# Modulation products moved to other stages of a two-block network

## The chip, the cores and the metric

One core of a Trainium2 chip runs the whole program in one launch. The metric is the device time of the kernel in microseconds, lower is better; the median of three runs is given. A trace comes from one profiled execution.

## The reference

Two blocks of a network run one after the other on x, 256 tokens by 2048, all in float32. The first has two layers: differential attention and, after a shared K and V product, forgetting attention. The second is a state-space (S5) mixer with a gate and an MLP with squared relu. What is moved here is the *modulation*: a vector c goes through silu and is multiplied with a large matrix, and slices of the result shift, scale and gate the tokens.

```
c_act = jax.nn.silu(c)
for l in range(DEPTH):                                  # 2 layers
    mod = c_act @ w_mod[l] + b_mod[l]                   # [2048] @ [2048, 6144]
    shift, scale, gate = jnp.split(mod, 3, axis=-1)
    h = x * (1.0 + scale[:, None]) + shift[:, None]
    if l < N_A:
        y = diff_attention(h, a_w_in[l], a_w_out[l], ...)
    else:
        k_sh, v_sh, F_sh = shared_kv(x, c_act, kv_w_mod, kv_b_mod, kv_w, kv_b_f)
        y = forgetting_attention(h, b_w_in[l - N_A], b_w_out[l - N_A], k_sh, v_sh, F_sh)
    x = layer_norm(DN_ALPHA * x + gate[:, None] * y, ln_g[l], ln_b[l])
...
sh1, sc1, gt1, sh2, sc2, gt2 = adaln(c, w_mod[layer], b_mod[layer])    # [2048] @ [2048, 12288], second block
```

## The kernel before

**Modulation.** All modulation matrices together are cut into 56 pieces of 2048 x 512 weights, 4 MiB each, listed in MODS in the order in which they are used: m0s (0 to 7), m2a (8 to 15), m0g (16 to 19), m1s (20 to 27), kv (28 to 35), m1g (36 to 39), m2b (40 to 51), m2c (52 to 55). One piece is one call of mod(j), which exists in four programs. SP loads it as four quarters of 1 MiB. TensorE (line 2064) first calls sums(j - 1), which reduces the row that ScalarE copied for the piece before into the bank MB0, and then multiplies the four quarters with the padded vector cpad, 32 records in the trace, each quarter as it lands. ScalarE (line 974) copies the bank into mod_rows. When a group is complete, VectorE adds its bias (mod_bias, line 1412), after a wait for the group's last sums.

**The ring.** All weights of the kernel pass through a ring of six slots of 1 MiB. The table made by tables() gives every load its slot in one fixed order; SP issues the loads in that order, and before each it waits until TensorE has used up the slot's last contents (place, line 597). So at most six quarters are ahead of TensorE, and a load that stands early in the order holds up those behind it.

**The stages around the change**, in order of time:
- Projections and state matrices, until about 738 us in the trace.
- The first attention block (lines 2308 to 2340): a software pipeline of 21 stages t over 16 tiles. In stage t TensorE multiplies a tile's weights with v (ao, tile t - 5), turns them (at, tile t - 4) and makes the scores (as, tile t); VectorE and ScalarE make the softmax between. It begins with loads of the projections that the kernel itself stored earlier (proj_d, 2 MiB each): 0 and 1 before it (lines 639, 640), 2 and 3 (lines 645, 650) after waits of SP on semaphores of small stores by GpSimd and on TensorE. VectorE starts when the last store of m_state has landed. The result is normed per head and turned (to_T, transposes on TensorE).
- Steps 0 to 3 (the product with a_w_out), then the first layer norm on VectorE, and steps 4 to 19 (q, g, k, v). A step is multiply(n): 4 MiB of weights in four quarters, split by ScalarE and VectorE into a high and a low part (w_hi, w_lo), and 96 matmuls of 128x512. Inside step 0 VectorE waits for x, which GpSimd loads once oT has been turned. After the layer norm GpSimd stores x (2 MiB, line 825), and TensorE turns it for step 4 (turn_in).
- The second attention block, steps 20 to 23, the second layer norm.
- The v stage (lines 2413 to 2418): 16 loads of 1 MiB of m_state through the ring, 8 chunks for each half f; ScalarE copies each chunk's result out (v_out). Then, for each f, a scan of 32 states on VectorE, each copied by ScalarE (states_out, line 1196).
- The y stage on TensorE (from line 2421), and the steps of the gated product and the MLP.

**Where mod(j) is called** is given by the dictionaries of lines 67 to 73: after a projection panel, after a chunk of the state matrices, in stage t of the first attention (MOD_AT_A), after step n (MOD_AT_STEP), at the layer norms (MOD_AT_LN), after each half of the v stage (MOD_AT_V) and in the second attention (MOD_AT_B). SP, ScalarE and TensorE follow the same dictionaries in their programs.

Of the kernel before, what the change touches and what calls it, by code (L numbers as in the profile page):

```python
# [60 lines left out]
MOD_END = {g: max(j for j, (h, _) in enumerate(MODS) if h == g) for g, _ in MODS}  # L61
# [4 lines left out]

MOD_AT_PRE = {**{pn: 8 + pn for pn in range(8)}, 9: 16, 11: 17}
MOD_AT_BL = {0: 18, 9: 19, 10: 20, 19: 21, 20: 22}
MOD_AT_A = {5: 23, 9: 24, 13: 25}
MOD_AT_STEP = {0: 26, 1: 27, 2: 28, **{n: 26 + n for n in range(4, 17)}, 55: 52, 56: 53, 57: 54, 58: 55}  # L70
MOD_AT_LN = ((29,), (48, 49))
MOD_AT_V = (50, 51)
MOD_AT_B = {2 + 6 * i: 43 + i for i in range(5)}
SUMMED = ("m0s", "m2b", "m2c")


# [12 lines left out]
N_Q, N_K, N_W1, N_GLU, N_MLP, NS = 4, 12, 20, len(FRONT), len(FRONT) + len(GLU), len(STEPS)  # L89
# [19 lines left out]
def tables():  # L109
# [8 lines left out]
    def mod(j):  # L118
        load("mod", j)
        bank.use(("mod", j), GM)  # L120
# [97 lines left out]
    for f in range(2):  # L218
        for i in range(8):
            ring.use(("ms", f, i), slots)  # L220
            bank.use(("vl", f, i), GV)
        mod(MOD_AT_V[f])
    for f in range(2):
        for i in range(8):
            ring.use(("cl", f, i), slots, 2)
# [18 lines left out]
def build(nc, A, out):  # L244
    ctx = ExitStack()
    with ctx:
# [77 lines left out]
        def reg(off, n):  # L324
            return AR[:, off:off + n]
# [267 lines left out]
        def sync_program(sp):  # L593
# [20 lines left out]
            def mod(j):  # L614
                load_w(("mod", j), MOD_W[MODS[j][0]], 0, 128 * MODS[j][1])
# [22 lines left out]
            sp.wait_ge(*filled("proj", 15, 1))  # L638
            sp.dma_start(reg(24576, 4096), proj_d[0]).then_inc(S["p0"], 16)
            sp.dma_start(reg(12288, 4096), proj_d[1]).then_inc(S["p1"], 16)  # L640
            sp.wait_ge(S["st0"], 16 * 8)
            sp.wait_ge(S["st1"], 16 * 8)
            sp.wait_ge(S["st2"], 16 * 8)
# [4 lines left out]
            sp.wait_ge(S["st2"], 16 * 10)  # L648
            sp.wait_ge(S["blm"], 32)
            sp.dma_start(reg(4096, 4096), proj_d[3]).then_inc(S["p3"], 16)  # L650
            for t in sorted(MOD_AT_A):
                mod(MOD_AT_A[t])

            W_OF = {"wout0": (A["a_w_out"][0], 0), "q": (A["b_w_in"][0], 0), "g": (A["b_w_in"][0], 2048), "k": (A["kv_w"], 0),
# [33 lines left out]
            for f in range(2):  # L688
                for i in range(8):
                    dst, sem = place("ms", f, i)  # L690
                    d0 = 64 * (i // 4) + 32 * f + 8 * (i % 4)
                    sp.dma_start(dst, m_state_d[:, d0 * 256:d0 * 256 + 2048]).then_inc(sem, 16)
                mod(MOD_AT_V[f])
            sp.wait_ge(S["cl0"], 16 * 16)
            sp.wait_ge(S["cl1"], 16 * 16)
            sp.wait_ge(S["toep"], 16 * 64)
# [146 lines left out]
        def scalar_program(a):  # L843
# [130 lines left out]
            def mod(j):  # L974
                a.wait_ge(*filled("mod", j))
                if j:
                    a.wait_ge(S["mod_sum"], j)
                copy(ROWS[:, :], bank("mod", j)[:, :], *empty("mod", j))
# [132 lines left out]
            for t in range(21):  # L1111
                if 0 <= t - 5 < 16:
                    i = t - 5
# [7 lines left out]
                if 0 <= t - 1 < 16:  # L1121
                    i = t - 1
# [31 lines left out]
            for t in range(35):  # L1154
                if 0 <= t - 2 < 32:
                    i = t - 2
# [5 lines left out]
                if 0 <= t - 1 < 32:  # L1162
                    i = t - 1
# [50 lines left out]

            for i in range(8):
                v_step(0, i)
            mod(MOD_AT_V[0])
            states_out(0, lambda i: v_step(1, i), 3)
            mod(MOD_AT_V[1])
            states_out(1, lambda i: y_step(0, i), 4)  # L1220
            for i in range(0, 8, 2):
                y_step(1, i)
# [60 lines left out]
        def vector_program(v):  # L1283
# [501 lines left out]
            for t in range(21):  # L1785
                if 0 <= t - 3 < 16:

                    i = t - 3
# [8 lines left out]
                if 0 <= t - 4 < 16:  # L1797
                    i = t - 4
# [5 lines left out]
                if 0 <= t - 1 < 16:  # L1804
                    i = t - 1
# [49 lines left out]
            v.wait_ge(S["x1"], 16)  # L1855
            v.wait_ge(*emptied("bc", "m0g", 3))
            for n in range(N_W1):
                if n == N_Q - 1:
                    mod_bias("m1s")
                if n == N_Q:  # L1860
                    layer_norm(0)
                    own()
                    ts(sc1, M("m1", 16), 1.0, None, ADD, None, *o.up("scol"))
                    split_in("q", h_raw["q"], sc1, M("m1", 0), AHk, ALk, N_Q, 8 * n)
                    scan_ctx(2)
                elif n == N_K:
                    v.wait_ge(*emptied("xt", "q", 7))
                    v.wait_ge(*filled("step", N_K - 1, 1))
                    own()
                    ts(sc1, M("kv", 16), 1.0, None, ADD, None, *o.up("scol"))  # L1870
                    split_in("k", h_raw["k"], sc1, M("kv", 0), AHk, ALk, N_K)
                    v.wait_ge(*filled("zf"))
                    v.wait_ge(S["zf"], 32)
                    tt(zz, bank("zf")[:, 0:32].rearrange("p (t h) -> p t h", t=2), bf.unsqueeze(1).to_broadcast([128, 2, 16]), ADD,
                       *empty("zf"))
                    own()
                    ts(tz, zz, -1.0, None, MUL, None)
                    own()
                    tt(tz, tz, zz, MIN, *o.up("zt"))
                    ts(lf, zz, 0.0, None, MIN, None)  # L1880
                    v.wait_ge(S["zl"], 1)
                    own()
                    tt(lf, lf, tz, SUB, *o.up("lf"))
                round_of(n, n in (N_Q - 1, N_W1 - 1))
                if n == N_K - 2:
                    mod_bias("kv")
                elif n == N_K + 2:
                    mod_bias("m1g")
            v.wait_ge(*filled("nFT"))
            ts(nFT[0:16, :], bank("nFT")[0:16, 0:256], -1.0, None, MUL, None, *empty("nFT"))  # L1890
# [2 lines left out]
            for t in range(35):  # L1893
                if 0 <= t - 3 < 32:
                    i = t - 3
# [8 lines left out]
                if 0 <= t - 1 < 32:  # L1904
                    i = t - 1
# [129 lines left out]
        def tensor_program(p):  # L2035
# [15 lines left out]
            def sums(j):  # L2051

                group, nt = MODS[j]
                p.wait_ge(*emptied("mod", j))
                ended = sum(1 for g_ in MOD_GROUPS if MOD_END[g_] < j)
                if j == MOD_FIRST[group] and ended:
                    p.wait_ge(S["mod_bias"], ended)
                c_ = mod_c(j)
                for i in range(4):
                    c0 = 256 + 2 * (nt + i) if group == "m2a" else mod_base(j) + i  # L2060
                    t = mm(MB0[:, c0:c0 + c_.stop - c_.start], ROWS[:, 128 * i:128 * i + 128], sel[:, c_], True, True)
                t.then_inc(S["mod_sum"], 1)

            def mod(j):

                if j and j - 1 not in [MOD_END[g_] for g_ in SUMMED]:
                    sums(j - 1)
                for q in range(4):
                    w = chunk("mod", j, q)
                    p.wait_ge(*landed("mod", j, q))  # L2070
                    if q == 0:
                        room("mod", j)
                    for i in range(4):
                        t = mm(bank("mod", j)[32 * i:32 * i + 32, :], cwide[:, 4 * q + i, :], w[:, i, :], q == 0, q == 3)
                    t.then_inc(*(fill("mod", j) if q == 3 else (S["taken"], 1)))
# [109 lines left out]
            for j in range(8):  # L2185
# [4 lines left out]
                if j == 4:  # L2190
                    p.wait_ge(S["lam_cols"], 1)
                    room("lam")
                    for i, s_ in enumerate((cr, ci, lbr, lbi)):
                        t = tr(bank("lam")[:, 128 * i:128 * i + 128], s_)
# [55 lines left out]
            def u_sums(run):  # L2250

                room("ss", run)
                if run == 0:
                    p.wait_ge(S["sq"], 1)
                    p.wait_ge(S["sq_even"], 1)
                    mm(bank("ss", 0)[:, 0:8], sel[:, :], ssu, True, True).then_inc(*fill("ss", 0))
                else:
                    p.wait_ge(S["ss_rows"], 2)
                    for t2 in range(2):
                        t = mm(bank("ss", 1)[:, 0:8], to_chunk[:, t2].rearrange("p a t c -> p (a t c)"), ss_rows[:, t2, :],  # L2260
                               t2 == 0, t2 == 1)
                    t.then_inc(*fill("ss", 1))
# [4 lines left out]
            for b in range(8):  # L2267
                t = mm(bank("fu")[:, 64 * b:64 * b + 64], spread[:, b, :, :].rearrange("p q h -> p (q h)"), u_cols, True, True)
# [21 lines left out]
            for b in range(33):  # L2290
                if b < 32:
                    p.wait_ge(S["blm"], b + 1)
                    for r in range(2):
                        room("bl", b, r)
                        for j in range(4):
                            t = tr(bank("bl", b, r)[:, 128 * j:128 * j + 128], bls[b % 2][r][:, 128 * j:128 * j + 128])
# [13 lines left out]
            for t_ in range(21):  # L2310
                if 0 <= t_ - 5 < 16:
                    i = t_ - 5
# [5 lines left out]
                    for s in range(t2 + 1):  # L2318
                        t = mm(bank("ao", i)[:, 0:256], a_av(i)[:, 128 * s:128 * s + 128], vN[0][:, s, 256 * h:256 * h + 256],
                               s == 0, s == t2)  # L2320
                    t.then_inc(*fill("ao", i))
                if 0 <= t_ - 4 < 16:
                    i = t_ - 4
                    p.wait_ge(S["amix"], i + 1)
                    room("at", i)
                    for s in range(i % 2 + 1):
                        t = tr(bank("at", i)[:, 128 * s:128 * s + 128], wk[i % 4][:, 128 * s:128 * s + 128])
                    t.then_inc(*fill("at", i))
                if t_ < 16:
# [3 lines left out]
                    for c in range(2):  # L2333
                        t = mm(bank("as", t_)[:, 256 * c:256 * c + w_], qT[0][:, 2 * h + c, 128 * t2:128 * t2 + 128],
                               kT[0][:, 2 * h + c, 0:w_], True, True)
# [37 lines left out]
            for t_ in range(35):  # L2373
                if 0 <= t_ - 3 < 32:
                    i = t_ - 3
# [30 lines left out]
                multiply(n)  # L2406
            for j in MOD_AT_LN[1]:
                mod(j)
            u_sums(1)
            for pc in range(8):  # L2410
                u_turn(1, pc)
            p.wait_ge(S["u_made"], 16)
            for f in range(2):
                for i in range(8):
                    p.wait_ge(*landed("ms", f, i))
                    v_chunk(("vl", f, i), slot("ms", f, i).rearrange("p (d r m) -> p d r m", d=8, r=2), UL,
                            64 * (i // 4) + 32 * f + 8 * (i % 4))
                mod(MOD_AT_V[f])
            sums(MOD_END["m2b"])
            p.wait_ge(S["zeroed"], 1)  # L2420
            for f in range(2):
                p.wait_ge(S["copied"], 32 * (f + 1))
# [90 lines left out]
```

## Time and profile before

| | us |
|---|---|
| Median of three runs | 2861.78 (2855.18 to 2862.5) |
| The profiled execution's own time | 2862.5 |
| Its span in the trace | 2860.7 |
| TensorE busy | 2583.2 (90%) |
| VectorE busy | 1578.2 (55%) |
| ScalarE busy | 1098.3 (38%) |
| Moved by DMA | 699.74 MB, 245 GB/s on average |

The shares are averages over stages that differ: what counts for a moved piece of work is what bounds the stage that it leaves and the stage that it enters.

### The profile page before, as it was taken

The page shows a single profiled execution, that of the slowest core. Times are in us where ns is not written, and L with a number is a line of the kernel's source. Part 1 is how long each engine was busy: PE and PEld are TensorE (multiplying, and loading weights), DVE is VectorE, ACT ScalarE, POOL GpSimd, SP SyncE. Part 2 cuts the span into 40 slices and gives each one's busy share as a digit, 9 for nine tenths or more (in the row PEclk, how much of TensorE's full clock was granted, in tenths as well). Part 3 has the DMA queues.
Part 4 walks back from the last instruction along what each step waited for, and adds up shares of the span by engine and source line. Part 5 has one row for each costly group of instructions (what it writes and reads, how often), then busy time and mean ns, then how long its engine had stood idle before and what let it go on. Part 6 is the DMA issues. An engine that isn't in the chain of part 4 may idle for free.

```text
span 2860.7 us, 42569 instructions
## 1 busy us (share of the span) xinstructions
PE 2583.2 (90%) x17983; PEld 2098.0 (73%) x17983; DVE 1578.2 (55%) x2434; ACT 1098.3 (38%) x1812; POOL 196.9 (7%) x299
## 2 busy tenths in 40 slices
PE   5799999888779799899999877889699999999997
PEld 1588877666557687797757666678598898998885
DVE  4566887788557754333335627354555455554444
ACT  0253333344432333334324327344444443443333
POOL 1112333010100001111000010000000000000000
PEclk8799999899889899899978957999899999999998
DMA  9979999675958689689655687745445555556852
GB/s 354 338 240 332 351 329 323 238 283 214 370 191 310 226 296 345 241 309 347 204 200 197 198 274 277 262 147 176 147 133 191 189 180 191 190 182 234 298 192 82
DMA packets 316574, 699.74 MB, mean 245 GB/s; under 512 B 13568, under 2 KB 14048, under 8 KB 311136
## 3 DMA queue, kind: packets, MB, share of 16 engines
q1 hardware_dynamic: 296992, 625.17, 63.1%
q0 software_dynamic: 19120, 69.75, 7.3%
q8 instruction: 142, 2.33, 0.3%
q10 hardware_dynamic: 272, 2.10, 0.2%
q14 instruction: 48, 0.39, 0.0%
HBM read 646.77 MB, written 56.49 MB: 246 GB/s over the span
## 4 chain that ended last, share of the span: by engine, by line
PE 74%; DVE 12%; DMA 8%; ACT 3%; issue 1%; SPq 1%; DVEq 0%; POOL 0%; ACTq 0%
PE bank L2037 72%; DVE arena L1287 4%; DMA ring<-in_a_w_in 3%; DMA ring<-in_w_mod 3%; DVE ring_lo L1287 2%; PE bank L2040 1%; DVE arena L1295 1%; ACT arena L850 1%; DVE sm L1287 1%; PE bank L2246 1%; DMA ring<-in_a_w_out 1%; DMA arena<-arena 0%; SPq L608 0%; DMA proj<-sm 0%; DMA arena<-in_x 0%
## 5 line engine op out<-in xcount | busy, mean ns | idle before, releaser
L1287 DVE TENSOR_TENSOR ring_lo<-ring,w_hi 128x1024 fp32r<-128x1024 f32 (+1 forms) x384 | 430.9, 1134 | 480.9 <-ACT w_hi L900 455.9
L900 ACT CAST w_hi<-ring 128x1024 fp32r<-128x1024 f32 x320 | 333.5, 1048 | 492.9 <-PE bank L2037 437.5
L1287 DVE TENSOR_TENSOR ring_lo<-ring,att_w_hi 128x1024 fp32r<-128x1024 f32 x192 | 231.0, 1222 | 299.1 <-ACT att_w_hi L900 289.7
L900 ACT CAST att_w_hi<-ring 128x1024 fp32r<-128x1024 f32 x192 | 197.5, 1048 | 380.7 <-PE bank L2037 125.7
L2037 PE MATMUL bank<-in_hi,w_hi 128*128 128x256 f32 x1024 | 290.9, 284 | 1.2 <-DVE n L1292 1.2
L2037 PE MATMUL bank<-in_lo,w_hi 128*128 128x256 f32 x1024 | 290.6, 284 | 0.0
L2037 PE MATMUL bank<-in_hi,ring_lo 128*128 128x256 f32 x1024 | 290.1, 283 | 0.0
L2037 PE MATMUL bank<-ring,cpad 128*32 128x512 f32 x1792 | 244.4, 682 | 28.4 <-DMA ring<-in_w_mod 24.8
L2037 PE MATMUL bank<-w_hi,hid_lo 128*128 128x512 f32 x640 | 257.7, 403 | 3.5 <-DVE ring_lo L1287 3.5
L2037 PE MATMUL bank<-att_w_hi,att_hi 128*128 128x512 f32 x512 | 206.1, 403 | 12.8 <-DVE ring_lo L1287 12.8
L2037 PE MATMUL bank<-ring_lo,att_hi 128*128 128x512 f32 x512 | 202.7, 396 | 0.0
L2037 PE MATMUL bank<-att_w_hi,att_lo 128*128 128x512 f32 x512 | 202.0, 395 | 0.0
L2037 PE MATMUL bank<-w_hi,hid_hi 128*128 128x512 f32 x512 | 201.6, 394 | 0.0
L2037 PE MATMUL bank<-ring_lo,hid_hi 128*128 128x512 f32 x512 | 200.7, 392 | 0.0
L2037 PEld LDWEIGHTS bank<-in_hi,w_hi 128*128 128x128 f32 x1024 | 195.8, 191 | 4.1 <-issue 2.5
L850 ACT CAST in_lo<-ring 128x512 fp32r<-128x512 f32 x192 | 115.4, 622 | 213.1 <-DMA ring<-in_a_w_in 107.2
L2037 PEld LDWEIGHTS bank<-in_hi,ring_lo 128*128 128x128 f32 x1024 | 195.4, 191 | 0.0
L2037 PEld LDWEIGHTS bank<-in_lo,w_hi 128*128 128x128 f32 x1024 | 194.9, 190 | 0.1
L2037 PEld LDWEIGHTS bank<-ring,cpad 128*32 128x32 f32 x1792 | 53.4, 119 | 164.9 <-issue 97.8
L2037 PE MATMUL bank<-w_hi,in_hi 128*128 128x512 f32 x384 | 153.8, 401 | 16.7 <-DVE in_lo L1287 14.4
L1287 DVE TENSOR_TENSOR ring_lo<-ring,in_lo 128x512 fp32r<-128x512 f32 x192 | 129.4, 702 | 70.2 <-ACT in_lo L850 70.0
L2037 PE MATMUL bank<-hid_lo,in_lo 128*128 128x256 f32 x512 | 149.8, 293 | 14.4 <-DVE ring_lo L1287 14.4
(249 smaller groups left out, 5103.2 us busy)
## 6 DMA issues: line engine op xcount, KB each, us to landing
ring<-in_w_mod SPq DMA_DIRECT2D x192, 1024.0 KB, 11.5
ring<-in_a_w_in SPq DMA_DIRECT2D x64, 1024.0 KB, 10.4
ring<-in_w_mlp_in SPq DMA_DIRECT2D x64, 1024.0 KB, 5.3
ring<-in_w_mlp_out SPq DMA_DIRECT2D x64, 1024.0 KB, 5.1
ring<-in_kv_w_mod SPq DMA_DIRECT2D x32, 1024.0 KB, 10.6
ring<-in_b_w_in SPq DMA_DIRECT2D x32, 1024.0 KB, 7.0
ring<-in_kv_w SPq DMA_DIRECT2D x32, 1024.0 KB, 6.8
ring<-in_s_w_glu SPq DMA_DIRECT2D x32, 1024.0 KB, 5.3
```

The lines of the kernel that those rows point to most:

```text
L850: return a.copy(dst, src).then_inc(*(to or o.up("act")))
L900: a.copy(whi(h), raw_half(h)).then_inc(*o.up("whi"))
L1287: return v.tensor_tensor(dst, x, y, op).then_inc(*(to or o.up("dve")))
L1295: return v.scalar_tensor_tensor(out=dst, in0=x, scalar=s1, in1=y, op0=o1, op1=o2).then_inc(*(to or o.up("dve")))
L2037: return p.matmul(dst, l_, r_, start=start, stop=stop, skip_group_check=True)
L2040: return p.transpose(dst, src, ident[0:k, 0:k])
L2246: t = p.transpose(bank("u", run, pc)[:, 32 * j:32 * j + 32], HT[run][at, e, j, :, :].rearrange("p q h -> p (q h)"), ident[at, at])
```

## The change

Which stages call mod(j) is changed. The attention block has six of them (23 to 28) in place of three (23 to 25), steps 0 to 2 have none in place of one each, the first layer norm has three (29 to 31) in place of one (29), and the v stage none in place of two. All later places keep their count and take an index that is higher by two, until the second layer norm, which has 50 and 51. SP issues the loads of mod 23 before those of projections 2 and 3. The biases of m1s, kv and m1g are added after earlier steps, and the last sums of m2b are made before u_sums(1).

```diff
-MOD_AT_A = {5: 23, 9: 24, 13: 25}
-MOD_AT_STEP = {0: 26, 1: 27, 2: 28, **{n: 26 + n for n in range(4, 17)}, 55: 52, 56: 53, 57: 54, 58: 55}
-MOD_AT_LN = ((29,), (48, 49))
-MOD_AT_V = (50, 51)
-MOD_AT_B = {2 + 6 * i: 43 + i for i in range(5)}
+MOD_AT_A = {1: 23, 4: 24, 6: 25, 9: 26, 11: 27, 14: 28}
+MOD_AT_STEP = {**{n: 28 + n for n in range(4, 17)}, 55: 52, 56: 53, 57: 54, 58: 55}
+MOD_AT_LN = ((29, 30, 31), (50, 51))
+MOD_AT_B = {2 + 6 * i: 45 + i for i in range(5)}
...
             sp.dma_start(reg(24576, 4096), proj_d[0]).then_inc(S["p0"], 16)
             sp.dma_start(reg(12288, 4096), proj_d[1]).then_inc(S["p1"], 16)
+            mod(MOD_AT_A[1])
             sp.wait_ge(S["st0"], 16 * 8)
...
-            for t in sorted(MOD_AT_A):
+            for t in sorted(MOD_AT_A)[1:]:
                 mod(MOD_AT_A[t])
...
-                mod(MOD_AT_V[f])
...
-            mod(MOD_AT_V[0])
             states_out(0, lambda i: v_step(1, i), 3)
-            mod(MOD_AT_V[1])
             states_out(1, lambda i: y_step(0, i), 4)
...
-                if n == N_Q - 1:
+                if n == 1:
                     mod_bias("m1s")
...
-                if n == N_K - 2:
+                if n == N_Q + 4:
                     mod_bias("kv")
-                elif n == N_K + 2:
+                elif n == N_Q + 8:
                     mod_bias("m1g")
...
             for j in MOD_AT_LN[1]:
                 mod(j)
+            sums(MOD_END["m2b"])
             u_sums(1)
...
-                mod(MOD_AT_V[f])
-            sums(MOD_END["m2b"])
```

## Rows read from the trace of the kernel before

**Rows 1.** The page: the span, and the chain that ended last by engine.
```profile
span 2860.7 us, 42569 instructions
...
PE 74%; DVE 12%; DMA 8%; ACT 3%; issue 1%; SPq 1%; DVEq 0%; POOL 0%; ACTq 0%
```

**Rows 2.** Windows: stretch, length, busy us (x instructions) by engine, PE clock, DMA, GB/s.
```profile
core 0: us, PE busy (x) PEld busy (x) DVE busy (x) ACT busy (x) POOL busy (x), PEclk, DMA share, GB/s
...
748.00:789.00 41.00, 37.79 (x226) 23.79 (x226) 27.13 (x91) 23.30 (x86) 0.00 (x0) 0.92 1.05 384
797.00:815.00 18.00, 12.64 (x64) 10.46 (x63) 14.44 (x34) 8.72 (x20) 0.00 (x0) 0.81 0.00 0
849.00:876.00 27.00, 26.68 (x136) 19.40 (x135) 19.86 (x30) 8.24 (x9) 0.00 (x0) 1.00 0.88 313
932.00:947.00 15.00, 4.21 (x39) 1.49 (x38) 13.87 (x20) 0.99 (x3) 0.00 (x0) 0.72 0.95 331
```

**Rows 3.** Timeline of SP's issues: start, length, what.
```profile
718.00 0.35 SPq L639 DMA_DIRECT2D arena<-proj  x1
...
734.48 37.37 SPq L608 DMA_DIRECT2D ring<-in_w_mod  x12
```

**Rows 4.** DMA view: the total of 718 to 748; slices of 748 to 796.
```profile
DMA packets 1506, 11.27 MB, mean 376 GB/s; under 512 B 159, under 2 KB 159, under 8 KB 993
...
GB/s 406 403 386 387 387 387 386 389 384 386 389 387 386 389 384 386 389 387 389 386 389 389 386 386 387 386 389 386 387 382 230 394 396 405 394 387 384 389 386 280
```

**Rows 5.** Timeline of the first attention block: start, length, engine, what, idle before.
```profile
747.66 0.42 DVE L1295 SCALAR_TENSOR_TENSOR LT<-LT,bank 128x256 f32<-128x256 f32 x1 [15.68 <-DMA m_state<-MSB]
...
759.49 1.06 PE L2037 MATMUL bank<-ring,cpad 128*32 128x512 f32 x8 [0.73 <-DMA ring<-in_w_mod]
...
768.54 0.95 PE L2037 MATMUL bank<-sel,mod_rows 128*128 128x1 f32 x8
...
781.04 0.95 PE L2037 MATMUL bank<-sel,mod_rows 128*128 128x1 f32 x8
...
787.11 0.70 PE L2037 MATMUL bank<-arena,MSB 128*128 128x256 f32 x2
...
807.24 2.79 PE L2040 MATMUL bank<-ident,arena 128*128 128x128 f32 x12 [4.47 <-DVE arena L1295]
```

**Rows 6.** Timeline of TensorE: the mods after steps 0 to 3, the turn.
```profile
848.96 0.95 PE L2037 MATMUL bank<-sel,mod_rows 128*128 128x1 f32 x8
849.84 3.64 PE L2037 MATMUL bank<-ring,cpad 128*32 128x512 f32 x32
...
876.43 0.95 PE L2037 MATMUL bank<-sel,mod_rows 128*128 128x1 f32 x8
...
903.75 0.95 PE L2037 MATMUL bank<-sel,mod_rows 128*128 128x1 f32 x8
...
931.63 0.95 PE L2037 MATMUL bank<-sel,mod_rows 128*128 128x1 f32 x8
...
946.94 5.80 PE L2040 MATMUL bank<-ident,arena 128*128 128x128 f32 x28 [10.79 <-DVE arena L1295]
```

**Rows 7.** Timeline of TensorE: the two mods of the second layer norm.
```profile
1626.40 0.95 PE L2037 MATMUL bank<-sel,mod_rows 128*128 128x1 f32 x8
...
1634.89 1.07 PE L2037 MATMUL bank<-ring,cpad 128*32 128x512 f32 x8 [0.36 <-DMA ring<-in_w_mod]
1638.22 1.94 PE L2037 MATMUL bank<-ring,cpad 128*32 128x512 f32 x8 [2.27 <-DMA ring<-in_w_mod]
```

**Rows 8.** DMA queues of 826 to 836, GpSimd's (q0) and SP's (q1).
```profile
q0 software_dynamic: 398, 3.08, 75.9%
q1 hardware_dynamic: 479, 0.95, 25.5%
```

**Rows 9.** Timeline around the v stage: ScalarE's copies, the sums before the y stage.
```profile
1702.32 1.02 ACT L850 COPY arena<-bank 128x256 f32<-128x256 f32 x2 [2.36 <-PE bank L2037]
1710.63 0.58 ACT L850 COPY mod_rows<-bank 128x512 f32<-128x512 f32 x1 [7.28 <-PE bank L2037]
...
1754.56 1.87 PE L2037 MATMUL bank<-sel,mod_rows 128*128 128x1 f32 x8 [13.16 <-ACT mod_rows L850]
```

More of the change, by code:

```diff
@@ L2417, in tensor_program @@
                             64 * (i // 4) + 32 * f + 8 * (i % 4))
-                mod(MOD_AT_V[f])
-            sums(MOD_END["m2b"])
             p.wait_ge(S["zeroed"], 1)
```

## The prediction

> **What bounds the kernel now.** I read the page first: the span is 2860.7 us, and its chain of work that ended last is 74% TensorE and 8% transfers [rows 1]. So a stage of this kernel is bound either by TensorE or by the loads that feed the ring, and each place that the change touches has to be asked which. The windows view answers it [rows 2]. In the first attention block (748 to 789) the DMA share is 1.05 at 384 GB/s: saturated. From 797 to 815 it is 0.00: the ring is full and nothing may be loaded. In a wout0 step (849 to 876) TensorE is busy 26.68 of 27 us with the DMA at 0.88. In the layer norm (932 to 947) TensorE is busy 4.21 of 15 us, but the DMA share is 0.95. I then took the DMA issues [rows 3], the totals moved [rows 4] and the TensorE timelines [rows 5 to 7, 9] for the terms.
>
> A *mod* (one call of mod(j)) is 4 MiB of weights, 4.19 MB, through four ring slots, and on TensorE 32 records in 3.64 us plus the column sums of the mod before in about 0.9 us: 4.5 us at the full clock [rows 6]. At the rate of 748 to 796, where nearly every slice shows 386 to 389 GB/s [rows 4], its load takes 4.19/0.387 = 10.8 us. A moved mod is therefore worth 4.5 us where TensorE is the bound and costs 10.8 us where the transfers are. That asymmetry is the argument.
>
> **The change part by part.** The total of work stays; 56 mods before and after. Three leave steps 0 to 2 for the attention block (3 become 6), two leave the v stage and are added to the first layer norm (1 becomes 3), and in steps 4 to 16, in the second attention and in the second layer norm every place keeps its count, with other indices. The three mod_bias calls keep or widen their distance to the sums they wait for, so VectorE gets no new wait; they cost nothing as long as the sums precede them, and each is one small operation.
>
> *Attention block.* From 718, where SP issues the first proj load [rows 3], the engine of the stage is the DMA. Until mod(28) has landed it must move four proj loads (8.39 MB), the writes of GpSimd (2.31 MB seen on its queue until 748) and six mods (25.17 MB): 35.9 MB. By 748 it had moved 11.27 MB [rows 4], and issuing mod 23 earlier cannot raise that, since the queue was already full. The other 24.6 MB take 24.6/0.387 = 63.6 us: 811.6. The same working for mod 23 before gives 757.4 (8.39 + 2.31 + 4.19 = 14.9 MB, less 11.27, by 0.387, from 748), and TensorE began its last quarter at 759.49, released by that transfer [rows 5]: 2.1 us of latency. So mod(28)'s last quarter is there at 813.7 and its matmuls end at 814.6. Is TensorE at each mod in time to free the slots? Stages between mods run at (781.04 - 768.54 - 4.5)/4 = 2.0 us each [rows 5], so two or three stages and a mod take 8.5 to 10.5 us, less than 10.8: the DMA stays the bound, without gaps. After the mod comes stage 15. Before, stage 15 began at 787.11 and the turn of oT at 807.24 [rows 5]; that tail of 20.1 us stays, because six more stages and the norm depend on each other. Turn at 834.7: +27.5 us. Ends: the pipeline may have worked ahead in the waits by one or two stages (+24), or the queue may have gaps (+29.5). wout0's first loads land at about 816 and later, behind 20 us of tail. Mod 23 ahead of proj 2 and 3 costs nothing here: if it delayed the small writes that release VectorE (it started at 747.66, released by one [rows 5]) by its own 10.8 us, attention would start at 758, still before mod 24, which by the same working (8.39 + 2.31 + 8.39 = 19.1 MB) lands at 770.
>
> One rule of the Trainium skill is weighed against this rate. The slices show 387 GB/s [rows 4]. "DMA: Bandwidth & Descriptors", section Bandwidth, gives 425 GB/s for one large load on a single core; by that the 24.6 MB would take 57.9 us, the stage would lose 21.8 instead of 27.5 us, and the whole sum would be +10.7. It would change the size and not the sign.
>
> *Steps 0 to 3.* The wait inside step 0 for x stays, since x is asked for when oT is turned. The distances between the sums at the ends of steps 0 to 3 are 27.47, 27.32 and 27.88 us [rows 6]; without their mods three times 4.5 us fall away, 13.6, and at most another 1.0 of small waits behind late quarters of the ring. I take -14.1 (ends -13.6 and -14.6). VectorE was busy 19.86 us in such a step [rows 2], below the new 22.8, so it doesn't become the bound.
>
> *First layer norm.* Before, one mod ran in 4.5 us and TensorE then idled 10.79 us until the norm was done, 946.94 - 931.63 = 15.3 us after the step's end [rows 6]. Three mods would fit by their TensorE time (13.6 us and two short waits for ScalarE's copy). But six slots hold the first mod and half of the second; the rest is loaded during the norm. The second layer norm shows exactly this: from the step's end at 1626.40 the second mod's third quarter was there after 8.5 us and its fourth after 11.8 [rows 7]. The third mod's four quarters follow at 1.049/0.387 = 2.7 us each: 22.7 us. At 15.3 the norm also starts the 2 MiB store of x, and where such a transfer of GpSimd's met ring loads it took 3.08 MB to their 0.95 [rows 8]; it holds them up by at most its own 5.4 us: 28.1, and with the last matmuls 29.2. TensorE's turn of x stands behind the mod in program order, and behind that turn ScalarE and VectorE wait for operands and step 4. The cost is between 23.8 - 15.3 = 8.5 and 13.9 us; 7.3 if the first quarters are a little earlier. I take +13, near the end where the store goes first. What is late next is step 4's own first load, one quarter behind, but it has the whole turn of x to land in.
>
> The same page of the Trainium skill ("DMA: Bandwidth & Descriptors", section Queues, rings and completion order) says that the engines go round robin between queues packet by packet. It fits that the store takes most of the rate; by equal shares the delay would be 5.4 us just the same, because both finish later than the store.
>
> *V stage.* ScalarE ended its last copy of v at 1703.34, waited 7.28 us for mod(50) and copied its row until 1711.2; only then did the states start. Without it they start at 1703.4: -7.8. The second row copy (0.58 like the first) and the sums at 1754.56 (1.8 us, half clock) go from the chain too [rows 9]. The sums move to the second layer norm, where TensorE idles. Sum -10.2, and up to 2 may be lost again to a colder array at the start of the y stage; I take -10.
>
> Sum: +27.5 - 14.1 + 13 - 10 = +16.4 us. The profiled execution took 2862.5 us; it becomes 2878.9. That execution stands 0.7 us above the median of the runs, 2861.78, so for the median I predict 2878. All low ends give +24 - 14.6 + 7.3 - 10.2 = +6.5, all high ends +29.5 - 13.6 + 13.9 - 8.2 = +21.6. A measurement of this kernel can tell about 0.3%, 8.6 us, from no change.
>
> **Rivals.**
> 1. *The loads find room (faster).* The three new mods cost the attention block only their TensorE time, 3 x 4.5 = +13.6, because the empty DMA stretch (797 to 815) takes them. With the rest as above that is 13.6 - 14.1 + 13 - 10 = +2.5, and if the layer norm's idle time hides its mods too, as the idle 10.79 us suggest, 13.6 - 14.1 + 0 - 10 = -10.5: 2851. For it speaks the hole in the DMA; against it that the hole comes after the block's last mod, and that the mods would have to land with 24.6 MB moved by 797.7, at 495 GB/s, where the rate stood flat at 387. It decides from a total below zero, that is, when the attention block and the norm together lose less than 24.1 us. Chance 0.1.
> 2. *The layer norm hides its mods, the attention does not (about the same).* +27.5 - 14.1 + 0 to 3 - 10 = +3.4 to +6.4: 2866. It needs the ring to be ahead at the norm; the second layer norm speaks against it. Chance 0.17.
> 3. *Late small writes open a gap.* Mod 23 ahead delays the two writes on which proj 3 hangs, SP stands in front of all other mods, and the DMA runs empty: up to 10.8 us more, 2889. The queue then still holds mod 23 and proj 2, 6.3 MB or 16 us, so it hardly empties. Chance 0.05.
> 4. My forecast, including its ends: 0.68.
>
> **How the numbers follow.** Cases 3 and 4 are slower, except the lowest corner of 4: 0.72. Case 2 lies within 0.3% (with some of that corner), 0.17, and case 1 is mostly faster: 0.11. The range goes down to 2860, into rival 2 and some of rival 1, and up to 2888.
>
> **What would show it.** In the changed profile: TensorE's mod groups of the attention block each with idle time released by the DMA of in_w_mod, about 10.8 us apart, the last near 813; the turn of oT near 835; three steps of 22.8 us; the third mod of the layer norm ending 24 to 29 us after step 3, with its last quarter released by a transfer; the states of the v stage starting within 1 us of ScalarE's last copy. The prediction is wrong if the block's mods land closer than 10 us apart, if the tail after the last is well under 20 us, or if the turn of x still starts 15 us after step 3.

## The result, and the profile after

| | before | after |
|---|---|---|
| Median of four runs, us | 2862.14 (2855.18 to 2864.38) | 2878.86 (2878.11 to 2882.5) |
| The profiled execution's own time | 2862.5 | 2882.47 |
| Its span | 2860.7 | 2880.7 |
| TensorE busy | 2583.2 (90%) | 2597.3 (90%) |

The ratio is 1.0065, with a 95% interval of 1.0046 to 1.0085: slower by 0.65%, or 16.7 us between the medians. 2878 was predicted, inside a range of 2860 to 2888.

The page of the changed kernel shows little. The first line below is its list of engines in the chain that ended last, then come the most important lines of that chain, and the group of the mods' matmuls: in_kv_w_mod is new among the lines of the chain, and TensorE's idle time ahead of mod matmuls is 57.2 us, 42.4 of it released by loads of in_w_mod.

```profile
PE 75%; DVE 11%; DMA 9%; ACT 2%; issue 2%; SPq 1%; DVEq 0%; POOL 0%; ACTq 0%
PE bank L2033 73%; DVE arena L1283 4%; DMA ring<-in_w_mod 4%; DMA ring<-in_a_w_in 3%; DVE ring_lo L1283 2%; PE bank L2036 1%; DMA ring<-in_kv_w_mod 1%; PE bank L2242 1%; DVE arena L1291 1%; SPq L606 1%; DMA arena<-arena 0%; DVE MSB L1283 0%; DMA arena<-in_x 0%; DVE y_mlp L1291 0%; DVE arena L1288 0%
L2033 PE MATMUL bank<-ring,cpad 128*32 128x512 f32 x1792 | 250.4, 690 | 57.2 <-DMA ring<-in_w_mod 42.4
```

So I cut both executions at events that they have in common. The columns are the two profiled executions and two more, taken later one after the other on one chip; the term is what the prediction gave.

| stretch (us) | before | after | before, again | after, again | term |
|---|---|---|---|---|---|
| SP's first proj load to the turn of oT | 89.24 | 114.91 | 87.90 | 114.95 | +27.5 |
| to TensorE's first product after the wait for x | 29.07 | 28.00 | 29.24 | 30.05 | 0 |
| to the end of step 3 | 95.32 | 80.98 | 95.73 | 79.10 | -14.1 |
| to the first product of step 4 | 28.04 | 42.61 | 28.03 | 40.38 | +13 |
| to the end of step 23 | 666.73 | 674.60 | 671.59 | 667.02 | 0 |
| to the start of v | 48.36 | 48.35 | 48.33 | 48.33 | 0 |
| to the start of y | 81.60 | 71.11 | 80.86 | 71.16 | -10 |
| to the start of z | 90.05 | 90.61 | 89.73 | 90.09 | 0 |
| to the end | 1014.29 | 1016.30 | 1015.08 | 1014.22 | 0 |

Four of the nine lines hold the change, and each came out within 2.6 us of its term, in both pairs.

**Attention block.** The timeline of TensorE in the changed kernel, start and duration in us and in brackets the idle time before with its releaser. These are the first quarter of mod 24 (755.60), for which TensorE waits 8.50 us, the last quarters of mods 24 to 27 (763.79 to 796.40), mod 28, the turn of oT, and the first product after x; [rows 5] is the same of before.

```profile
755.60 1.93 PE L2033 MATMUL bank<-ring,cpad 128*32 128x512 f32 x8 [8.50 <-DMA ring<-in_w_mod]
763.79 1.93 PE L2033 MATMUL bank<-ring,cpad 128*32 128x512 f32 x8 [0.87 <-DMA ring<-in_w_mod]
774.64 1.06 PE L2033 MATMUL bank<-ring,cpad 128*32 128x512 f32 x8 [0.41 <-DMA ring<-in_w_mod]
785.45 1.06 PE L2033 MATMUL bank<-ring,cpad 128*32 128x512 f32 x8 [0.88 <-DMA ring<-in_w_mod]
796.40 1.61 PE L2033 MATMUL bank<-ring,cpad 128*32 128x512 f32 x8 [1.65 <-DMA ring<-in_w_mod]
805.60 3.64 PE L2033 MATMUL bank<-ring,cpad 128*32 128x512 f32 x32
828.14 2.79 PE L2036 MATMUL bank<-ident,arena 128*128 128x128 f32 x12 [4.46 <-DVE arena L1291]
856.14 0.79 PE L2033 MATMUL bank<-att_w_hi,att_hi 128*128 128x512 f32 x1 [11.77 <-DVE ring_lo L1283]
```

The last quarters of the mods are 10.85, 10.81 and 10.95 us apart, for the 10.8 worked out from the rate, and each is released by a transfer. The windows of the changed kernel, with the columns of [rows 2], say the same: the block moves 389 GB/s with a DMA share of 1.04 while TensorE is busy 34.16 of 48 us and has the clock 0.79. In the steps (891 to 914) TensorE is busy all the time and the DMA share is 0.55, for 0.88 in a step with its mod [rows 2]. In the layer norm (937 to 967) the share is 0.99 and TensorE is busy 17.45 of 30 us.

```profile
748.00:796.00 48.00, 34.16 (x203) 16.56 (x203) 16.00 (x54) 15.79 (x56) 0.00 (x0) 0.79 1.04 389
891.00:914.00 23.00, 23.00 (x100) 18.52 (x99) 20.46 (x31) 8.39 (x8) 0.00 (x0) 1.00 0.55 189
937.00:967.00 30.00, 17.45 (x122) 5.30 (x120) 14.41 (x21) 1.58 (x4) 0.54 (x1) 0.78 0.99 368
```

**Layer norm.** TensorE's timeline from the end of step 3 (937.12) to step 4. The first mod runs at once (938.00 x32), the second and third come quarter by quarter, and the turn of x (967.00), which had waited 10.79 us for VectorE [rows 6], now stands ready behind the third mod and has no idle time before it.

```profile
937.12 0.95 PE L2033 MATMUL bank<-sel,mod_rows 128*128 128x1 f32 x8
938.00 3.64 PE L2033 MATMUL bank<-ring,cpad 128*32 128x512 f32 x32
946.85 1.06 PE L2033 MATMUL bank<-ring,cpad 128*32 128x512 f32 x8 [1.60 <-DMA ring<-in_kv_w_mod]
954.99 1.93 PE L2033 MATMUL bank<-ring,cpad 128*32 128x512 f32 x8 [1.60 <-DMA ring<-in_kv_w_mod]
961.34 1.93 PE L2033 MATMUL bank<-ring,cpad 128*32 128x512 f32 x8 [4.42 <-DMA ring<-in_kv_w_mod]
965.14 1.93 PE L2033 MATMUL bank<-ring,cpad 128*32 128x512 f32 x8 [1.87 <-DMA ring<-in_kv_w_mod]
967.00 3.25 PE L2036 MATMUL bank<-ident,arena 128*128 128x128 f32 x14
979.73 0.55 PE L2033 MATMUL bank<-att_hi,att_w_hi 128*128 128x256 f32 x1 [2.33 <-issue]
```

**V stage.** ScalarE's timeline: the last copy of v at 1730.25 and, right behind it, the first copies for the states. The 7.28 us of [rows 9] are gone.

```profile
1730.25 1.05 ACT L848 COPY arena<-bank 128x256 f32<-128x256 f32 x2 [2.37 <-PE bank L2033]
1731.10 1.84 ACT L848 COPY arena<-BBD 64x64 f32<-64x64 f32 x8
```

### The profile page after: what moved, and what is told of

Its sections match the earlier page's. It is cut to its first block, busy times and chain, and to the rows that moved or that the text cites. A ratio compares the mean times of both kernels' runs of the same rounds, so it can differ in the third digit from the quotient of the medians.

```text
span 2880.7 us, 42569 instructions
## 1 busy us (share of the span) xinstructions
PE 2597.3 (90%) x17983; PEld 2106.5 (73%) x17983; DVE 1577.9 (55%) x2434; ACT 1099.5 (38%) x1812; POOL 195.8 (7%) x299
## 4 chain that ended last, share of the span: by engine, by line
PE 75%; DVE 11%; DMA 9%; ACT 2%; issue 2%; SPq 1%; DVEq 0%; POOL 0%; ACTq 0%
PE bank L2033 73%; DVE arena L1283 4%; DMA ring<-in_w_mod 4%; DMA ring<-in_a_w_in 3%; DVE ring_lo L1283 2%; PE bank L2036 1%; DMA ring<-in_kv_w_mod 1%; PE bank L2242 1%; DVE arena L1291 1%; SPq L606 1%; DMA arena<-arena 0%; DVE MSB L1283 0%; DMA arena<-in_x 0%; DVE y_mlp L1291 0%; DVE arena L1288 0%
## 5 line engine op out<-in xcount | busy, mean ns | idle before, releaser
L2033 PE MATMUL bank<-ring,cpad 128*32 128x512 f32 x1792 | 250.4, 690 | 57.2 <-DMA ring<-in_w_mod 42.4
L2033 PE MATMUL bank<-w_hi,in_hi 128*128 128x512 f32 x384 | 155.1, 404 | 16.4 <-DVE in_lo L1283 14.4
L2033 PE MATMUL bank<-hid_lo,in_lo 128*128 128x256 f32 x512 | 148.9, 291 | 14.6 <-DVE ring_lo L1283 14.6
## 6 DMA issues: line engine op xcount, KB each, us to landing
ring<-in_a_w_in SPq DMA_DIRECT2D x64, 1024.0 KB, 10.6
ring<-in_kv_w_mod SPq DMA_DIRECT2D x32, 1024.0 KB, 10.6
```

Of the source, the lines that this page charges most:

```text
L2033: return p.matmul(dst, l_, r_, start=start, stop=stop, skip_group_check=True)
```

## The experiments

Each kernel stands against runs of the kernel before on the same chip (medians 2863.91 and 2864.9, of 22 and 28 runs), and each trace was cut at the same events.

### The attention part alone

```
-MOD_AT_A = {5: 23, 9: 24, 13: 25}
-MOD_AT_STEP = {0: 26, 1: 27, 2: 28, ...}
+MOD_AT_A = {1: 23, 4: 24, 6: 25, 9: 26, 11: 27, 14: 28}      # norm, v stage: as before
```

> Only the part of the change at the attention block: six mods there (23 to 28), none in steps 0 to 2, mod 23 issued early; one mod at the first layer norm and two in the v stage, as before. Theory (the loads bound the block): from the first proj load to the turn of oT about 115 us against 89.2 before, steps 0 to 3 shorter by 14 us, so +10 to +12 us in all, near 2873. Rival (the block has room, and the loss of the whole change lies at the layer norm): block +14 us or less, total within 2 us of before, 2862.

Median 2879.16, ratio 1.0052 (1.0037 to 1.0068). The block took 115.18 us (before 89.24) and the steps 80.28 (95.32): +25.9 - 15.0 = +10.9 by the stages, while layer norm and v stage kept their times (28.02 and 81.66). The ratio gives +14.9 us (10.6 to 19.5), and the rest is in the stretch from step 4 to 23, whose work is unchanged: 675.64 us. A second execution had 115.07, 80.10 and 672.37 there. So the steps pay back little more than half of what the block loses.

### The norm and v stage part alone

```
 MOD_AT_A, steps 0 to 2: as before
+MOD_AT_LN = ((29, 30, 31), (50, 51))        # and no MOD_AT_V
```

> Only the part at the layer norm and the v stage: three mods (29 to 31) at the first layer norm, none in the v stage; the attention block and steps 0 to 2 as before. Theory: the turn of x starts 28 to 30 us after the end of step 3 in place of 15.3, the states start 7.8 us earlier and the y stage 10.5 us earlier: +4 us, near 2866. Rival (the layer norm's idle time hides the mods): -8 to -10 us, near 2853.

Median 2871.08, ratio 1.002 (1.0011 to 1.003). From step 3 to step 4 it took 41.57 us (before 28.04), in the v stage 71.15 (81.60): +13.5 - 10.4 = +3.1. TensorE's timeline: step 3 ends at 932.77, the last quarter waits 5.55 us for its transfer, and the turn of x starts 29.05 us after the step.

```profile
932.77 0.95 PE L2032 MATMUL bank<-sel,mod_rows 128*128 128x1 f32 x8
959.96 1.94 PE L2032 MATMUL bank<-ring,cpad 128*32 128x512 f32 x8 [5.55 <-DMA ring<-in_kv_w_mod]
961.82 3.35 PE L2035 MATMUL bank<-ident,arena 128*128 128x128 f32 x15
```

The ratio gives +5.7 us (3.2 to 8.6), at whose low end the +3.1 of the stages lies. The norm does not hide its mods, which refutes rival 2 (it wanted 0 to 3 us here). The two halves of the change give 1.0052 and 1.002, the whole 1.0065: within their intervals they add up.

### Mod 23 issued ahead, nothing else

```
             sp.dma_start(reg(12288, 4096), proj_d[1]).then_inc(S["p1"], 16)
+            mod(MOD_AT_A[min(MOD_AT_A)])           # MOD_AT_A = {1: 23, 9: 24, 13: 25}
             sp.wait_ge(S["st0"], 16 * 8)
```

> Before, with one edit: the loads of mod 23 are issued before projections 2 and 3, and TensorE does it in stage 1 instead of stage 5. Theory (the queue is full either way): 0, within 3 us of before, VectorE's start in the block no later than before. Rival (late small writes): the start of VectorE and the two proj loads come up to 10.8 us later, total up to +10 us.

Median 2862.34, ratio 0.9993 (0.9984 to 1.0002): no difference that can be told. The first line below is SP's proj load, the second VectorE's start, released by the last small store.

```profile
713.95 0.35 SPq L639 DMA_DIRECT2D arena<-proj  x1
739.12 0.42 DVE L1296 SCALAR_TENSOR_TENSOR LT<-LT,bank 128x256 f32<-128x256 f32 x1 [11.18 <-DMA m_state<-MSB]
```

VectorE starts 25.2 us after the proj load, where it took 29.7 without the change [rows 3, 5]. The small writes land earlier with mod 23 in the queue, not later. SP did issue projections 2 and 3 later, as rival 3 had it (17.1 and 21.1 us after the first, for 15.4 and 15.9), but no gap followed, and the block takes 86.16 us, 1.7 to 3.1 less than in the two executions of before: rival 3 falls.

The DMA view shows what the last small store (512 KB, issued 18.4 us after the first proj load in both) had beside it. The first two lines are 736.5 to 747 of before, with proj loads on SP's queue (q1), the last two 732.5 to 739 of this kernel, with mod 23 there: packets, MB, share of the DMA.

```profile
q1 hardware_dynamic: 329, 3.70, 85.8%
q0 software_dynamic: 143, 0.52, 12.2%
q1 hardware_dynamic: 1066, 2.12, 84.2%
q0 software_dynamic: 149, 0.54, 20.2%
```

The same store landed 11.1 us after its issue beside packets of 11 KB on average, and 6.7 us beside packets of 2 KB.

### Half of the transfers in the block

Half of the weights of mods 24 to 28 is left out: each quarter loads and uses two of its four blocks of columns twice. TensorE's instructions stay the same in number and size.

```
+                if key[0] == "mod" and 24 <= key[1] <= 28:
+                    dst, src = dst[:, 0:2, :], src[:, 0:2, :]
...
-    t = mm(..., w[:, i, :], q == 0, q == 3)
+    t = mm(..., w[:, i % 2 if 24 <= j <= 28 else i, :], q == 0, q == 3)
```

> The changed kernel, but mods 24 to 28 load only half of each quarter (the first two of its four tiles, 10.5 MB less) and multiply those two tiles twice, so TensorE does the same number of matmuls; half of those modulation rows' weights is left out. Theory (the loads bound the block): the block falls from 115 us to what its own pipeline needs with three mods more on TensorE, 86.2 + 3 x 4.5 = 99.7 us, total -15 us against the changed kernel, near 2864. Rival (the longer block is TensorE's and the pipeline's own time): it stays at 115 us and the total at 2879.

Median 2868.38, ratio 1.0008 (0.9996 to 1.002): 2.3 us above before (-1.1 to 5.7), where the first sum of rival 1 had +2.5. The block took 101.48 us, against 114.91 with whole loads and 99.7 expected. Its timeline shows the mods of the block in one piece, with no wait for a transfer, and its window a DMA share of 0.86, TensorE busy 42.74 of 48 us and the clock 0.88:

```profile
768.09 3.64 PE L2036 MATMUL bank<-ring,cpad 128*32 128x512 f32 x32
795.87 3.64 PE L2036 MATMUL bank<-ring,cpad 128*32 128x512 f32 x32
818.44 2.79 PE L2039 MATMUL bank<-ident,arena 128*128 128x128 f32 x12 [4.48 <-DVE arena L1294]
```

```profile
748.00:796.00 48.00, 42.74 (x278) 25.45 (x274) 23.50 (x78) 23.21 (x83) 0.00 (x0) 0.88 0.86 312
```

That is before's 87.9 to 89.24 plus 12.2 to 13.6 us, the TensorE time of three mods. So rival 1's price (13.6 us) is about right for a block whose loads find room. With whole loads they don't: 13.4 us of the 25.7 that the block loses are owed to the bytes. How much of that is the wait itself and how much the lower clock beside it (0.79 against 0.88) was not taken apart.

### The store of x after the mods

GpSimd stores x once the matmuls of step 4 are done (at 1004.32 in its trace), instead of at the norm's end (952.67 in the changed kernel).

```
+            g.wait_ge(*filled("step", N_Q, 1))     # step 4, before GpSimd's store of x
```

> The changed kernel with GpSimd's store of x (2 MiB) held back until the matmuls of step 4 are done, so that it doesn't meet the loads of the layer norm's third mod. Theory (the store takes the rate from the ring): the turn of x starts 24.5 us after step 3 in place of 30, total -5.4 us against the changed kernel, near 2873. Rival (the store waits its turn or fits in gaps): no difference, 2879.

Median 2877.39, ratio 1.0045 (1.0029 to 1.0061). Step 3 ended at 943.56 and the turn of x began at 967.45, 23.9 us later instead of 29.88; the last quarter waited 0.78 us instead of 1.87. The second execution of the changed kernel had 28.47 us there, the norm part alone 29.05.

```profile
943.56 0.95 PE L2034 MATMUL bank<-sel,mod_rows 128*128 128x1 f32 x8
966.45 1.06 PE L2034 MATMUL bank<-ring,cpad 128*32 128x512 f32 x8 [0.78 <-DMA ring<-in_kv_w_mod]
967.45 1.53 PE L2037 MATMUL bank<-ident,arena 128*128 128x128 f32 x12
```

So the store costs the ring 4.6 to 6.0 us, and 23.9 is the prediction's own value without it (29.2 - 5.4 = 23.8). The stretch to step 4 took 35.34 us instead of 42.61 or 40.38. The total (1.0045 against 1.0065 for the whole change) moved by less than the two intervals.

The Trainium skill ("DMA: Bandwidth & Descriptors", section Queues, rings and completion order) has the engines go round robin between queues packet by packet. The trace of the changed kernel agrees. While both queues were busy (957 to 961) the store's (q0) and the ring's (q1) moved the same number of packets:

```profile
q0 software_dynamic: 96, 1.57, 91.7%
q1 hardware_dynamic: 96, 0.19, 12.5%
```

In bytes that is 1.57 MB against 0.19, because the store's packets have 16 KB and the ring's 2 KB. For the delay of the third mod this division does not matter, as the prediction said: the store had landed before the mod's last quarter, so all its bytes went ahead, 5.4 us by the ring's rate, 4.6 to 6.0 measured.

### The v stage's mods later, in place

The two mods stay between second attention and y stage, but TensorE does both after the two halves of v, and ScalarE copies their rows among its copies for the scan, where it waits for VectorE anyway. The last sums of m2b stand between the two halves of the y stage.

```
         for i in range(8): ...               # both halves f of v first
-        mod(MOD_AT_V[f])
+    for j in MOD_AT_V: mod(j)
-            mod(MOD_AT_V[0])
-            states_out(0, lambda i: v_step(1, i), 3)
+            states_out(0, lambda i: v_step(1, i), 3, 26, MOD_AT_V[0])    # copies the row at state 26
```

> Before, with only the v stage altered: mods 50 and 51 stand after both halves of the chunks on TensorE, ScalarE copies their rows inside the scans (after state 26 of the first, state 2 of the second), and the last sums stand between the halves of the y stage. No load moves to another stage. Theory (the 10.5 us of the v stage are the wait of ScalarE for the mod, not the mod's work): the y stage starts 7 to 8 us earlier, total -6 to -8 us, near 2855. Rival (TensorE's or the DMA's time is the price): 0 to -2 us.

Median 2858.06, ratio 0.9974 (0.9963 to 0.9986): faster. The stage took 72.76 us, 8.8 and 8.1 less than in the two executions of before, with no mod moved to the layer norm. ScalarE's states start at 1705.32, right behind the last copy of v:

```profile
1704.47 1.06 ACT L852 COPY arena<-bank 128x256 f32<-128x256 f32 x2 [2.40 <-PE bank L2039]
1705.32 1.85 ACT L852 COPY arena<-BBD 64x64 f32<-64x64 f32 x8
```

This was the good part of the change, and it needed an order, not another stage.

### One mod in the hole behind the block

Mod 26 leaves step 0 and runs after the 21 stages, ahead of the turn of oT, where TensorE waits for the norm [rows 5] and the DMA share is 0.00 [rows 2].

```
-MOD_AT_STEP = {0: 26, 1: 27, 2: 28, ...}
+MOD_AT_STEP = {1: 27, 2: 28, ...}
+    mod(26)                                  # after stage 20, before the turn of oT
```

> Before, with only mod 26 moved, from the end of step 0 to TensorE's idle 4.47 us before the turn of oT; its loads stand ahead of those of step 0 and fall into the stretch in which the DMA moved nothing. ScalarE copies its row after the rsqrt. Theory (a moved mod costs only where both TensorE and the DMA are free it costs nothing): the turn of oT stays at 89 us after the first proj load, within 1.5 us, and step 0 ends 4.5 us earlier: -4 us, near 2858. Rival (step 0's late quarters then bind): 0.

Median 2856.11, ratio 0.9975 (0.9962 to 0.9988). The first timeline row below is the sums ahead of mod 26, the last the turn of oT, 88.70 us after SP's proj load at 719.32, as before:

```profile
803.37 0.95 PE L2040 MATMUL bank<-sel,mod_rows 128*128 128x1 f32 x8
804.25 3.64 PE L2040 MATMUL bank<-ring,cpad 128*32 128x512 f32 x32
808.02 2.04 PE L2043 MATMUL bank<-ident,arena 128*128 128x128 f32 x12
```

From the proj load to the end of step 3 it took 207.4 us, against 213.6 and 212.9 in the two executions of before: 5.5 to 6.2 us gained for the 4.5 of the mod. The rest goes with the clock. Its window of the hole shows 1.00 where before has 0.81 [rows 2], and the first twelve transposes of the turn took 2.04 us instead of 2.79.

```profile
797.00:815.00 18.00, 16.35 (x107) 11.27 (x108) 15.01 (x34) 10.02 (x22) 0.00 (x0) 1.00 0.48 174
```

One mod fits in without a price; three, ahead of the block's end, do not.

### The three together

The v stage's mods in place, mod 26 in the hole and mod 23 issued ahead, in one kernel that takes nothing else from the change.

> The edits of v_late, pre_turn and early_only together. Theory: they lie in different stages and add up: -7 - 4 - 2 = -13 us against before, near 2850. Rival (they meet in the ring or at a common wait): less than the best of them alone, -8.

Median 2851.56 (2847.13 to 2853.92), ratio 0.9957 (0.9944 to 0.9969): 12.3 us faster than before (8.9 to 16.0), with its median 27 us below that of the change, or 31 by the two ratios. Alone the three gave 7.4, 7.2 and 2.0 us. Mod 23 ahead and mod 26 in the hole did not add up: the turn of oT came 89.16 us after the first proj load, as in before, where mod 23 alone had 86.16.

### The same kernels once more

> The changed kernel, profiled once more. Theory (chance): the stretch from step 4 to the end of step 23 differs from 674.6 us by several us, towards 670. Rival (the change makes it longer): 674 to 676 again.

The second executions of before, of the change and of the attention part alone took 2861.45, 2870.99 and 2871.84 us. The stretch from step 4 to the end of step 23 took 671.59, 667.02 and 672.37 us in them, where the first ones had 666.73, 674.60 and 675.64. So it differs by several us between executions of one kernel, in either direction, and the rival (the change makes it longer) falls. The change's 2870.99 lies below all four runs of the result (2878.11 to 2882.5); what makes up that difference was not traced further than in the table above.

## Why the prediction was right

**The asymmetry** (4.5 us where TensorE is the bound, 10.8 where the transfers are) was the whole argument, and it is shown from both sides: the mods land 10.81 to 10.95 us apart, and with half the bytes the block loses 12.2 to 13.6 us instead of 25.7 to 27.1.

**Attention block, +27.5, measured +25.7 and +27.1** in the two pairs. The point of the last mod was right: it ended 96.0 us after the proj load, where 96.6 was worked out. Mod 28 itself no longer waited, though (805.60 x32, no idle time ahead), since its quarters had landed while TensorE did the stages before it. The turn of oT followed 18.9 us after the mod's end instead of 20.1. The 4.77 us by which this execution reached the stage earlier (713.23 for 718.00) are none of the change's doing: the other kernels, whose code ahead of it is the same, reached it between 711.09 and 719.32.

**Mod 23 ahead, costed at nothing.** It earns a little: the same 4.5 us earlier start of VectorE stand in the changed kernel (738.36, 25.1 after the load). I took the early issue for harmless because it could only delay the writes. The runs show the reverse. In the place of mod 23, with its rows of 2 KB, the small writes had proj loads beside them, with packets of up to 16 KB. The rows of the two traces fit that as the reason (the same store landed after 11.1 and after 6.7 us), but no run changed the size of the packets alone.

**Steps, -14.1, measured -14.3 and -16.6.** The second is below the low end of -14.6; the wait for x ahead of it was 0.8 us longer in that pair, which takes part of it back. If the rest of step 0 took the 12.65 us that it took before (836.31 to 848.96), 68.3 us are left for the other three steps, 22.8 each as forecast. VectorE is busy 20.46 of 23 us in the window above, nearer to the bound than the 19.86 that the prediction took, but not past it.

**Layer norm, +13, measured +14.6 and +12.3.** In the profiled execution this is 0.7 above its high end, in the second 0.7 below the value taken. The turn of x began 29.88 and 28.47 us after the step's end where 29.2 was worked out; against the run with the late store that puts the store at 6.0 and 4.6 us, around the 5.4 of the prediction. So the term is off by no more than one execution differs from the next.

**V stage, -10, measured -10.5 and -9.7.**

**The total** was predicted as +16.4 and came as +16.7 between the medians, but part of that closeness is luck. In the profiled pair the four terms, +25.7, -14.3, +14.6 and -10.5, sum to +15.4 before rounding; in the second pair +27.1, -16.6, +12.3 and -9.7 sum to +13.1. The spans differ by 20.0 in the first pair and by 9.6 in the second. Most of what lies between is the stretch from step 4 to step 23, the same work in all kernels: +7.9 in the first pair and -4.6 in the second. In the first pair the -4.8 ahead of the block, -1.1 at x and +2.6 behind the v stage make up the rest. One pair of profiles would have made a cause of it.

Nearly all of it lies in the second attention block. These are its windows in the four executions (before, before again, after, after again), from TensorE's first instruction of the block to the first product of step 20:

```profile
1413.44:1536.73 123.29, 110.88 (x548) 67.79 (x547) 50.43 (x152) 40.31 (x117) 1.09 (x2) 0.75 0.56 200
1407.71:1536.77 129.06, 116.66 (x547) 70.56 (x547) 50.76 (x152) 40.36 (x117) 1.09 (x2) 0.72 0.54 191
1434.76:1565.50 130.74, 120.19 (x548) 73.07 (x547) 50.38 (x151) 40.45 (x117) 1.09 (x2) 0.69 0.53 188
1431.76:1555.73 123.97, 112.49 (x548) 69.01 (x547) 50.40 (x152) 40.42 (x117) 1.09 (x2) 0.74 0.55 199
```

The block does the same 547 or 548 matmul records each time and its time differs by +7.4 us in the first pair and -5.1 in the second. The longer it took, the lower was the granted clock, from 0.75 to 0.69. Time and clock go together here; that the clock is the cause was not tried.

**The rivals.** Rival 1 needed 495 GB/s and the block ran at 389. The Trainium skill ("DMA: Bandwidth & Descriptors", section Bandwidth) gives 425 GB/s for one large load on one core; by that, as an estimate, the block would have lost 21.8 us. It lost 25.7 and 27.1: for the ring's loads the trace doesn't bear the figure out, and the rate read from the stage itself does. It depends on what is in the queue. The first line is 740 to 748 of the changed kernel, with the end of the large proj loads among the ring's, the second 750 to 790, with packets of 2 KB nearly alone:

```profile
DMA packets 500, 3.45 MB, mean 432 GB/s; under 512 B 32, under 2 KB 32, under 8 KB 326
DMA packets 7567, 15.41 MB, mean 385 GB/s; under 512 B 237, under 2 KB 237, under 8 KB 7539
```

Rival 2 is refuted by the norm's part alone, rival 3 by mod 23 alone.

## What to carry to other kernels

Price moved work by what bounds the stage that it enters, bytes over the stage's own rate as well as engine time, and look where exactly a hole in a resource lies: the empty DMA stretch was 18 us long, but it came after the block that got the mods, and one mod put in it paid. An engine's idle time beside a long operation is no room for work whose bytes are not there; the ring holds one mod and a half, and only that much is free. Before moving work out of a stage that waits for it, try to reorder it in place.

## What the runs showed of the hardware

- The same code took 123.3 to 131.7 us in the second attention block over the thirteen executions, at a granted clock of 0.75 and 0.69 (the longest is the first of the attention part alone). What makes the clock differ between executions was not tried; a difference of 5 us there says nothing about a change.
- Small writes landed about 4.5 us sooner when ring loads of mod 23 were issued ahead of the later proj loads (VectorE, released by the last, started 25.2 and 25.1 us after the first proj load, against 29.7 and 29.5 in the two executions of before).
- A 2 MiB store issued by GpSimd took 4.6 to 6.0 us from the ring's loads; its bytes take 5.4 at the ring's rate. In 4 us with both queues busy each moved 96 packets, which were 1.57 MB of the store and 0.19 MB of the ring.
- The ring's loads in packets of 2 KB ran at 385 to 389 GB/s with the DMA saturated; 8 us in which larger packets were among them reached 432.
